# Eight groups of value-weight sums in a hybrid decoder layer: separate times for load, sums and store

## The reference

```python
h = rmsnorm(x, norm_w[layer])
proj = jnp.einsum('bsd,dp->bsp', h, w_in[layer])
qa, ka, va, ga, qb, kb, vb, gb = jnp.split(proj, SPLIT_IDX, axis=-1)
...
va = va.reshape(b, s_len, A_HEADS, A_VDIM)
...
oa = diff_attention(qa, ka, va, lam)
...
x = x + jnp.einsum('bsm,md->bsd', y, w_out[layer])
```

## Time and profile before

| | us |
|---|---|
| median of 3 runs | 1745.81 (1744.99 to 1749.72) |
| the profiled execution's own time | 1747.95 |
| its span, first to last instruction | 1746.1 |
| TensorE busy | 1725.7 |
| VectorE busy | 1297.2 |
| ScalarE busy | 843.1 |
| GpSimd busy | 465.7 |

### The profile page before, as it was taken

How to read it: one execution, slowest core, us unless ns; L and a number is a source line. 1 busy time by engine, 2 the same in 40 slices (tenths; PEclk the granted TensorE clock), 3 DMA queues, 4 the chain that set the end, 5 groups by cost and what they waited for, 6 DMA issues and landing times.

```text
span 1746.1 us, 28224 instructions
## 1 busy us (share of the span) xinstructions
PE 1725.7 (99%) x8720; PEld 1446.6 (83%) x8720; DVE 1297.2 (74%) x2601; ACT 843.1 (48%) x2209; POOL 465.7 (27%) x661
## 2 busy tenths in 40 slices
PE   9999999999999999999999999999999999999999
PEld 8877888888888888888888888888888878888887
DVE  7779787787878687878788675876867787455754
ACT  6322432556555555656555454544445467333321
POOL 3211000332424242423333332432423424210000
PEclk9999999999999999999999999999999999999999
DMA  6288344534444443444343343452443566597654
GB/s 227 69 274 277 107 114 129 150 111 130 124 133 130 135 125 125 140 128 137 119 141 115 106 132 122 120 165 84 133 136 107 188 216 215 175 318 237 205 195 157
DMA packets 265099, 268.54 MB, mean 154 GB/s; under 512 B 26914, under 2 KB 190754, under 8 KB 263970
## 3 DMA queue, kind: packets, MB, share of 16 engines
q1 hardware_dynamic: 264992, 267.23, 48.8%
q10 hardware_dynamic: 2, 0.01, 0.0%
HBM read 188.52 MB, written 80.74 MB: 154 GB/s over the span
## 4 chain that ended last, share of the span: by engine, by line
PE 66%; issue 12%; POOL 7%; DVE 6%; DMA 2%; ACT 1%; SPq 0%; POOLq 0%; DVEq 0%; ACTq 0%
PE ps_a L1442 15%; PE ps_a L1444 15%; PE ps_a L1443 14%; PE ps_b L1444 4%; PE ps_b L1442 4%; PE ps_b L1443 4%; PE ps_b L1611 2%; PE ps_a L1563 2%; PE ps_a L1562 2%; DVE attention_parts L1854 2%; PE ps_b L1626 1%; POOL ss_o L2455 1%; POOL ss_o L2451 1%; POOL stage_rows L2488 1%; POOL ss_h L2455 1%
## 5 line engine op out<-in xcount | busy, mean ns | idle before, releaser
L1442 PE MATMUL ps_a<-hT_hi,w_hi_sb 128*128 128x512 f32 x1280 | 523.3, 409 | 3.4 <-DVE w_lo_sb L1854 3.4
L1444 PE MATMUL ps_a<-hT_hi,w_lo_sb 128*128 128x512 f32 x1280 | 502.6, 393 | 0.0
L1443 PE MATMUL ps_a<-hT_lo,w_hi_sb 128*128 128x512 f32 x1280 | 499.7, 390 | 0.0
L1444 PEld LDWEIGHTS ps_a<-hT_hi,w_lo_sb 128*128 128x128 f32 x1280 | 240.6, 188 | 54.4
L1442 PEld LDWEIGHTS ps_a<-hT_hi,w_hi_sb 128*128 128x128 f32 x1280 | 241.6, 189 | 50.6 <-DVE w_lo_sb L1854 4.6
L1443 PEld LDWEIGHTS ps_a<-hT_lo,w_hi_sb 128*128 128x128 f32 x1280 | 241.9, 189 | 43.0
L1854 DVE TENSOR_TENSOR w_lo_sb<-w_raw_sb,w_hi_sb 128x512 fp32r<-128x512 f32 (+2 forms) x287 | 194.7, 680 | 110.6 <-ACT w_hi_sb L1093 56.0
L1854 DVE TENSOR_TENSOR ps_a<-ps_a,mask 128x128 f32<-128x128 f32 (+2 forms) x176 | 67.9, 397 | 121.3 <-PE ps_a L1563 121.2
L1093 ACT ACTIVATE w_hi_sb<-w_raw_sb 128x512 fp32r<-128x512 f32 (+1 forms) x220 | 123.9, 564 | 68.7 <-DMA w_raw_sb<-in_w_in 35.7
L1854 DVE TENSOR_TENSOR attention_parts<-ps_b,attention_parts 64x128 fp32r<-64x128 f32 (+4 forms) x304 | 130.7, 447 | 18.0 <-ACT attention_parts L1303 15.4
L1303 ACT ACTIVATE attention_parts<-ps_b 128x512 fp32r<-128x512 f32 (+3 forms) x160 | 76.3, 517 | 140.1 <-PE ps_b L1611 139.9
(11 more groups left out here) (190 smaller groups left out, 3496.7 us busy)
## 6 DMA issues: line engine op xcount, KB each, us to landing
w_raw_sb<-in_w_in SPq DMA_DIRECT2D x108, 256.0 KB, 3.0
w_out_sums<-in_w_out SPq DMA_DIRECT2D x64, 256.0 KB, 3.7
w_out_sums_dram<-w_out_sums SPq DMA_DIRECT2D x64, 256.0 KB, 2.6
w_raw_sb<-in_w_in SPq DMA_DIRECT2D x64, 192.0 KB, 2.6
qkv_sb<-qkv_a_dram SPq DMA_DIRECT2D x64, 192.0 KB, 2.6
w_out_sums<-y_dram SPq DMA_DIRECT2D x24, 512.0 KB, 4.6
qkv_a_dram<-stage_rows SPq DMA_DIRECT2D x40, 256.0 KB, 2.5
w_raw_sb<-w_out_sums_dram SPq DMA_DIRECT2D x40, 256.0 KB, 3.2
```

Source lines behind the costliest of these rows:

```text
L1442: pe.matmul(dst, a_hi, b_hi, start=start, stop=False)
L1443: pe.matmul(dst, a_hi, b_lo, start=False, stop=False)
L1444: return pe.matmul(dst, a_lo, b_hi, start=False, stop=stop)
```

## The change

The one table with fixed distances is replaced by three tables, one each for load, sums and store. Both halves of a group still stand in the same step. By step, before and in the change:

| group | load | sums | store |
|---|---|---|---|
| 0 | 0, 0 | 2, 3 | 3, 4 |
| 1 | 2, 1 | 4, 4 | 5, 5 |
| 2 | 4, 5 | 6, 7 | 7, 8 |
| 3 | 6, 6 | 8, 8 | 9, 9 |
| 4 | 8, 9 | 10, 11 | 11, 12 |
| 5 | 11, 10 | 13, 12 | 14, 13 |
| 6 | 12, 13 | 14, 15 | 15, 16 |
| 7 | 14, 14 | 16, 17 | 17, 18 |

```diff
--- before.py
+++ after.py
@@ -128,15 +128,17 @@
 V_LEFT_AT = {"A11": (0, 0), "A12": (HALF_K, 0), "A22": (HALF_K, 512)}
 V_T = {"T1": 0, "T3": 1, "T2": 3, "T4": 2}
 V_B = {"B11": (0, 0), "B21": (1024, 0), "B22": (1024, 512)}
-V_SUM_AT = [0, 2, 4, 6, 8, 11, 12, 14]
-
-
-def v_sum_steps(*delays):
-
-    return {t: [(kk, h) for kk in range(HALF_K) for h in range(2) if V_SUM_AT[kk] + delays[h] == t] for t in range(48)}
-
-
-V_SUM_LOADS, V_SUMS, V_SUM_STORES = v_sum_steps(0, 0), v_sum_steps(2, 2), v_sum_steps(3, 3)
+V_SUM_LOAD = [0, 1, 5, 6, 9, 10, 13, 14]
+V_SUM_AT = [3, 4, 7, 8, 11, 12, 15, 17]
+V_SUM_STORE = [4, 5, 8, 9, 12, 13, 16, 18]
+
+
+def v_sums_at(times):
+
+    return {t: [(kk, h) for kk in range(HALF_K) for h in range(2) if times[kk] == t] for t in times}
+
+
+V_SUM_LOADS, V_SUMS, V_SUM_STORES = v_sums_at(V_SUM_LOAD), v_sums_at(V_SUM_AT), v_sums_at(V_SUM_STORE)
 V_S1_AT = [1, 1, 4, 10, 11, 16, 17, 18]
```

## The result

The changed kernel took 1753.68 us in the median of 8 runs (1752.2 to 1754.77), the kernel before on the same chip 1747.08 (8 runs). The ratio is 1.0036, 95% interval 1.0027 to 1.0045: **slower, by about 6.3 us**. Forecast were 1748.1 us, with 1752.5 as the upper end, so the prediction was wrong. The span of the profiled execution is 1751.8 us against 1746.1.

A forecast was written before the change was run, and what follows sets the result against it. TensorE, busy 99% of 1746.1 us, bounds the kernel; only its waits can give. Gone 6.5 us, new 9.9, +3.4 less 1.1 of counting: +2.3 on the 1745.81 median, 1748.1 us; range 1742.5 to 1752.5.

The forecast's parts named there:

- Waits that go: Weight chunks c5 to c7: the 1.12 us wait before c5 goes; c7 starts at 104.1, a new 0.9 us.
- L2 and sum 2: Group 2's load lands at 112.4, its VectorE subtractions wait 1.7 us; weight chunk c10 starts at 116.4, costing 1.0 us.
- c11: Weight chunk 11: its residue, behind group 3's subtractions, is done at 122.7; TensorE waits 2.2 us.
- L4 and sum 4: Group 4's load lands at 131.0 to 131.5; VectorE idles 4.3 us; chunk c14's residue is in time.
- c15: Weight chunk 15: group 5's subtractions precede its residue, done at 144.5; TensorE waits 1.9 us.
- t1: Values' tile 1: residue done at 150.5, so the 3.17 us wait and 1.6 us of low clock go.
- count by VectorE alone: Up to tile t6: VectorE idle 11.1 us before, about 12.7 after; with rounding, +1.6 to +2.6 us.
- S7 and the last loads: Last store and tile loads: tile t7's residue is ready about 170.8, needed at 173, so hidden.
- The queue decides: Rival, chance 0.20: group 4's load lands after 133, behind a chunk load awaiting its residue; +6.3 us, 1752.1 us.
- Even trade: Rival, chance 0.14: loads of groups 2 and 4 take 4.8 us despite stores ahead; -0.8, 1745.0 us.
- The stalls only go: Rival, chance 0.08: no new waits, VectorE reaches tile t6 four to six us sooner; about -5, 1740.8 us.
- the +6.3 of the bounds: Slow end: every load pair costs 1 us per half more, loads of groups 2 and 4 come 2 us later each.

The follow-up runs named there:

- Run 7: The changed kernel with the loads of groups 2 and 4 one step earlier (steps 4 and 8): 1749.99 us, ratio 1.0011 to before.
- Run 1: The changed kernel with ScalarE making tile t1's high part ahead of the gate copies in step 15: 1753.82 us, ratio 1.0032 to before.
- run 3: The kernel before with the change for groups 4 to 7 alone: 1752.28 us, ratio 1.0027.
- run 11: The kernel before with attention_parts sums moved into steps where VectorE idles, and sum 0 in step 3: 1744.08 us, ratio 0.9985.
- run 13: The kernel before with sum 0 in step 3 and attention_parts sums in a second choice of steps: 1744.18 us, ratio 0.9982.
- run 4: The kernel before with only the sums and stores of groups 6 and 7 one step later: 1747.5 us, ratio 1.0001.
- run 15: The kernel of run 13 with sum 6 in step 15 instead of 14, its store in 16: 1746.86 us, ratio 0.9996 to before.
- run 6: The changed kernel with only the load of group 4 one step earlier (step 8): 1752.07 us, ratio 1.0023 to before.
- run 5: The changed kernel with only the load of group 2 one step earlier (step 4): 1751.39 us, ratio 1.0023 to before.
- run 2: The kernel before with the change for groups 0 to 3 alone: 1753.08 us, ratio 1.0038.
- run 8: The changed kernel with sum 5 back in step 13 and its store in 14: 1755.28 us, ratio 1.0048 to before.
- run 14: The changed kernel with attention_parts sums at steps 1, 1, 2, 2, 4, 9, 11, 12: 1755.13 us, ratio 1.0046 to before.

## Why the prediction was wrong, step by step

The result lies 1.2 us past the range's end, the difference to before is 6.3 us where 2.3 were forecast. By the trace, the miss at t6 is 3.1 to 3.4 us. Another 1.3 us of the miss in the time itself are no part of the change: the kernel before measured 1747.08 beside it, not the 1745.81 that the forecast added to.

1. *Waits that go.* Right: no wait before c5. c7 started at 103.09 after 1.55 us, forecast 104.1 after 0.9. In this trace c2 ran at the full clock, so c4 ended earlier; the forecast could not know this, and it was worth nothing, since c7's residue sets c7.
2. *L2 and sum 2.* Right: L2 issued at 104.51 (105.7), landed at 112.10 (112.4), sum 2 idle 2.22 us (1.7), c10 at 116.12 (116.4). The forecast's own terms, 0.4 + 3.0 + 3.0 + 2.5 us from 104.15, add up to 113.05, not 112.4, so it is nearer than its prices were; for L4 they give 132.0.
3. *c11.* Right: 122.15 after 1.66 us (122.7 after 2.2).
4. *L4 and sum 4.* Nearly: landed at 131.84 (131.0 to 131.5), idle 4.80 (4.3). c14 waits 0.45, forecast none.
5. *c15.* Right: it waits 1.89 us (1.9), from 145.07, 0.6 us late.
6. *t1.* **This is the step that failed.** The forecast had t1's residue done at 150.5, ahead of TensorE's need; it started at 153.59 and was done at 154.3. Two things are missing in it. First, t1's high part was taken as made long before, because in the earlier trace rows it was made at 146.90. But on ScalarE it stands behind the two copies that wait for c15's matmuls, the second for its end. Before, c15 began at 140.77 and the high part 6.1 us later; with c15 at 144.5, as forecast, that gives 150.6, and the residue after it. Second, the forecast let the low clock go with t1's wait. In this trace it came back on c15: 0.60 in 145 to 149 us, and t0 started 7.2 us behind c15 where the others without a low clock there have 5.4 to 5.6. So the copies came at 149.72 and 152.44, the high part at 152.93, and VectorE stood idle for 3.37 us just where the forecast had it full. From there to t6 all its work is a queue without gaps: t4's residue was done at 166.9 where 163.5 was forecast, and t6 started at 173.60 for 170.2 to 170.5. The forecast's count by VectorE alone had its idle time go from 11.1 to 12.7 us; by the waits above it went from 11.9 to 18.4 between 84 and 168 us.

   Other traces size the two. From c15 to t6 the forecast had 25.9 us and the change took 28.5. Run 7, with c15 at the full clock, took 26.9: **the low clock is 1.6 us**. Run 1, with ScalarE's order changed too, took 26.5, or 25.9 without the low clock behind its t4: **ScalarE's order is 1.0 us**. These are single traces. Run 1's median shows no gain, and the low clock on c15 was in part chance: the same wait of 1.89 us brought none in runs 1 and 3.
7. *S7 and the last loads.* Right: no tile waits for a load.

Steps 5 and 6 thus give 3.2 of the 4.0 us by which the difference was missed; the rest is within the interval of the ratio.

On the rivals. *The queue decides* named the time, 1752.1 us, but not the way: its sign was L4 landing after 133 us, and L4 landed at 131.84, as the forecast had it. That the queue is the larger part of the loss is shown all the same, by run 7: with the two loads earlier the waits before c7, c10 and c14 are gone and those before c11 and c15 smaller (1.15 and 1.43 us). The forecast had these waits and was short in what follows from them. *Even trade* fell: it wanted second halves of 4.8 us, and they took 6.67 and 7.17, the stores being ahead of them. The Trainium skill ("DMA: Bandwidth & Descriptors", section on queues, rings and completion order) does say that completion is not in order of issue for one issuing engine. In the traces of before and of the change all transfers that SyncE issued between 84 and 175 us landed in the order of issue; over all 17 traces 6 of 1080 landed ahead of an earlier one, by 0.8 us at most. But the same section of the Trainium skill also has each DMA engine take up its descriptors in ring order, so it does not say that L2 would be worked off ahead of S1: the sum of -0.8 hangs on the forecast's own reading of it, and is further from the result than the other. *The stalls only go* fell too, though its premise, idle VectorE time that could be used, is what runs 11 and 13 live on, with other work.

That the measured difference is just the +6.3 of the bounds is luck. That end was worked out for both load pairs at a higher price, which they did not have; nothing was in it for work that had been on time only by TensorE's earlier finish.

Open: how much of the 1.0011 of run 7 is the sums' order, and how many of the change's executions have the low clock on c15.

## What to carry over

Where loads and stores go through one queue, giving each its own time can move loads behind stores: here two loads came behind a chunk load and two stores each, and that was 4.4 of the 6.3 us (run 7). Before moving a side task out of a wait, ask where the engine has free time within reach: here a sum put off by a step only handed its wait to the next tile (runs 4 and 15), while work moved into the holes that late loads leave gained 0.15 to 0.18% (runs 11, 13). And when a walk through the queues delays the main engine, look at everything that another engine does *after a result of the main engine*: such work was early in the old trace only because the main engine was.

## What the runs showed of the hardware that was not expected

**The granted clock after equal waits differs from one execution to the next.** The kernel before waits 1.79 us before c2, at 81.87, and its windows then show

```profile
84.00:86.00 2.00, 2.00 (x6) 1.57 (x5) 1.90 (x4) 0.00 (x0) 0.00 (x0) 0.51 0.67 171
```

The changed kernel waits the same 1.79 us at the same matmul (81.69) and shows

```profile
84.00:86.00 2.00, 2.00 (x11) 1.65 (x10) 1.90 (x4) 0.00 (x0) 0.00 (x0) 1.00 0.74 192
```

0.51 is 1.2 GHz, 1.00 is 2.4 GHz; eleven matmuls fall into the stretch where six did, and c5 is reached 3.1 us earlier, of which only 1.12 are the wait that went. All 17 traces have this wait before c2, of 1.78 or 1.79 us; in ten c3 starts 5.8 us behind c2, in seven 4.2. The same wait of 1.89 us before c15 brought the low clock in the change and not in run 1, where 145 to 149 us show 1.00, nor in run 3. A wait of 2.32 to 2.36 us before t4 brought it in runs 1 and 6 and not in runs 3, 4, 5, 7 and the change. So the length of the wait alone does not fix where these 1.6 us fall. After longer waits the lower level was seen for longer in some traces: in run 2 the windows give 0.50 from 134 to 140 us and 0.95 in the two after, behind a wait of 3.53 us before c13; in run 8 (3.89 us before t3) 0.50 from 164 to 168 and 0.77 in the two after; in run 14 (4.54 us, the longest wait) only 0.51 and 0.64 in 148 to 152, then 1.00.

**One stopped load holds the whole queue.** 7.1 us of waiting for one store's landing delayed a tile load that had all it needed (run 8). **How long a transfer of 512 KB took, from issue to landing, went by what stood ahead of it.** The second half of L4 took 4.79 us before, with little ahead but its first half; in the change, behind a chunk load and the two stores of S3, 7.17 us, and that of L2 6.67. Over all 16 of these loads in the change the times are 4.1 to 8.3 us, over the 16 stores 3.1 to 6.0.
